# A diffusion backbone layer pair on one core: the feed-forward in two phases, statistics by token half, and seven block products for eight

## The reference, cut to what matters

```
x = x + gate1 * rmsnorm(mixer(modulate(rmsnorm(x))))        # mixer: attention or convolution module
h = modulate(rmsnorm(x))
u = depthwise_conv(h @ w_up, w_dw) + b_dw                   # w_up 1024 x 5632, 3 taps along the tokens
gate, val = split(u, 2)                                     # 2816 channels each
x = x + gate2 * rmsnorm((silu(gate) * val) @ w_down)        # w_down 2816 x 1024

# convolution module
u = a * sigmoid(g)          with a, g = split(h @ w_pw1 + b_pw1, 2)
u = silu(layernorm(depthwise_conv(u, 31 taps) + b_dw))
y = u @ w_pw2 + b_pw2
```

## Time and profile before

| | |
|---|---|
| median of 3 runs | 2824.36 us (2817.53 to 2825.59) |
| profiled execution, its own time | 2821.07 us |
| its span | 2819.3 us |
| PE busy | 2695.0 us, 96% |
| DVE busy | 1663.8 us, 59% |
| ACT busy | 854.7 us, 30% |
| POOL busy | 385.9 us, 14% |
| mean granted clock of PE | 0.976 |
| DMA | 193.96 MB, mean 69 GB/s |

### The profile page before, as it was taken

How to read it: one execution, slowest core, us unless ns; L and a number is a source line. 1 busy time by engine, 2 the same in 40 slices (tenths; PEclk the granted TensorE clock), 3 DMA queues, 4 the chain that set the end, 5 groups by cost and what they waited for, 6 DMA issues and landing times.

```text
span 2819.3 us, 31209 instructions
## 1 busy us (share of the span) xinstructions
PE 2695.0 (96%) x11986; PEld 2134.7 (76%) x11986; DVE 1663.8 (59%) x1770; ACT 854.7 (30%) x1102; POOL 385.9 (14%) x266
## 2 busy tenths in 40 slices
PE   6889999999999999999999999998999999999996
PEld 6667888887758888888887576655678888888884
DVE  5636676767356544554544789995374445444455
ACT  2224444445343222222222422216342222222221
POOL 0402140404025314040400100000100000000001
PEclk9989999999999999999999899999999999999998
DMA  6301120203323212131212200002121111111112
GB/s 245 105 16 50 45 73 21 74 15 109 133 95 112 83 67 97 60 104 52 89 45 104 82 30 30 30 30 82 41 80 60 45 52 45 52 45 52 45 51 106
DMA packets 55063, 193.96 MB, mean 69 GB/s; under 512 B 5840, under 2 KB 7120, under 8 KB 54992
## 3 DMA queue, kind: packets, MB, share of 16 engines
q1 hardware_dynamic: 28048, 99.07, 10.6%
q10 hardware_dynamic: 15424, 51.98, 4.8%
q0 software_dynamic: 11520, 41.95, 4.6%
HBM read 172.00 MB, written 20.97 MB: 68 GB/s over the span
## 4 chain that ended last, share of the span: by engine, by line
PE 89%; DVE 4%; issue 4%; ACT 2%; DMA 1%; POOL 0%; ACTq 0%; POOLq 0%; SPq 0%; DVEq 0%
PE psum L1227 25%; PE psum L1229 25%; PE psum L1228 25%; PE psum L1576 4%; PE psum L1248 2%; PE psum L1448 2%; PE psum L1438 1%; PE psum L1437 1%; PE psum L1235 1%; DVE f32r_region L797 1%; PE psum L1281 1%; DMA f_region<-ctx_t 1%; PE psum L1288 1%; DVE small L925 1%; PE psum L1424 1%
## 5 line engine op out<-in xcount | busy, mean ns | idle before, releaser
L1227 PE MATMUL psum<-f32r_region 128*128 128x512 f32 (+1 forms) x3288 | 1300.1, 395 | 48.9 <-DVE f32r_region L797 13.8
L1228 PE MATMUL psum<-f32r_region 128*128 128x512 f32 (+1 forms) x3288 | 1272.2, 387 | 0.0
L1229 PE MATMUL psum<-f32r_region 128*128 128x512 f32 (+1 forms) x3288 | 1272.0, 387 | 0.0
L1227 PEld LDWEIGHTS psum<-f32r_region 128*128 128x128 f32 x3288 | 624.8, 190 | 197.0 <-issue 32.3
L1228 PEld LDWEIGHTS psum<-f32r_region 128*128 128x128 f32 x3288 | 625.6, 190 | 125.8 <-issue 6.0
L1229 PEld LDWEIGHTS psum<-f32r_region 128*128 128x128 f32 x3288 | 624.6, 190 | 126.3
L384 ACT ACTIVATE f32r_region<-f_region 128x1024 fp32r<-128x1024 f32 (+1 forms) x251 | 254.3, 1024 | 498.1 <-PE psum L1229 446.1
L1095 DVE SCALAR_TENSOR_TENSOR f_region<-psum,vectors,f_region 128x1023 f32<-128x1023 f32 x88 | 112.8, 1282 | 492.3 <-ACT f_region L673 492.3
L673 ACT ACTIVATE f_region<-psum,vectors 128x1024 f32<-128x1024 f32 x88 | 106.2, 1207 | 589.2 <-PE psum L1229 589.2
L1112 DVE TENSOR_TENSOR f_region<-f_region,psum 128x1024 f32<-128x1024 f32 x160 | 194.8, 1217 | 145.9 <-PE psum L1229 145.9
L347 POOL TENSOR_TENSOR f_region<-f_region,f32r_region_plain 128x512 f32<-128x512 f32 x32 | 52.7, 1648 | 1522.8 <-DVE f_region L1055 1522.8
(11 more groups left out here) (108 smaller groups left out, 1853.9 us busy)
## 6 DMA issues: line engine op xcount, KB each, us to landing
f_region<-units SPq DMA_DIRECT2D x178, 512.0 KB, 3.5
f_region<-mod_w POOLq DMA_DIRECT2D x80, 512.0 KB, 3.9
residual<-f_region ACTq DMA_DIRECT2D x24, 512.0 KB, 4.9
f32r_region_plain<-residual ACTq DMA_DIRECT2D x24, 512.0 KB, 7.8
f32r_region_plain<-mod_w ACTq DMA_DIRECT2D x8, 1024.0 KB, 16.3
f_region<-x_t SPq DMA_DIRECT2D x4, 1024.0 KB, 27.9
heads_out<-f_region ACTq DMA_DIRECT2D x16, 256.0 KB, 2.1
f_region<-heads_out ACTq DMA_DIRECT2D x8, 512.0 KB, 4.3
```

The costliest lines, as they stand in the source:

```text
L1227: pe.matmul(out, wl, xh, start=first, stop=False)
L1228: pe.matmul(out, wh, xl, start=False, stop=False)
L1229: return pe.matmul(out, wh, xh, start=False, stop=last)
```

## The change: what it does

**Two phases.** All 22 pairs are made first, each gated block is stored to a tensor `gated` in HBM, and the down-projection follows in four turns: token half 0 with the first four output blocks, then with the last four, then the same for half 1. A turn has 22 steps `j` of 12 matmuls; the sums over `j` stay in PSUM, so DVE's adds (L1112) go. Half units of down weights (256 KB) are loaded in every turn, so each comes twice, and in turns 0 and 2 the gated block's half is read back and split into parts.

**Seven products for eight.** The first three pairs are made directly. For each of the other 19 (MAIN) the 2 x 2 blocks (gate and value rows by two halves of the input channels, on two token halves) are multiplied by seven products in place of eight, each of 4 x 3 matmuls, with sums of weights (s1 to s4, made by POOL for every pair) and of inputs (T1 to T4, made once a layer). PSUM banks a, b, c accumulate; what has to be added across banks is copied out by ACT after its product (`part`), and added by POOL and DVE. The taps of pair p-1 are done in period p, from SBUF.

**Statistics by token half** (`stat_cols`, `stat_spread`): squares of 128x512 are summed over blocks by POOL, and residual, scaling and parts of half 0 go beside PE's work on half 1. The mixers' output projections are made half by half for this, all 8 units of weights at once in SBUF. Modulation vectors are all made during attention, three in a loop trip.

**Convolution.** DVE's gating of the next block (L1189 before, `gated_block`) and the split of two units stand after the twelfth tap of a block, where they stood between two blocks. ACT's copy for the second chain still waits for the end of the block before.

The core of the diff:

```diff
+PRODUCTS = (("gate", 0, "a"), ("s2", 1, "b"), ("s1", 2, "c"), ("s3", 3, "b"), ("gate", 4, "a"), ("s4", 5, "c"), ("val", 6, "b"))
+BANKS = ({"a": 5, "c": 6, "b": 7}, {"a": 1, "c": 2, "b": 3})
...
         @block.gpsimd
+                x, y, op = {1: (a21, a22, ADD), 2: (f(to[0], HALF), a11, SUB), 3: (a11, a21, SUB), 4: (a12, f(to[1], HALF), SUB)}[part]
+                pool.tensor_tensor(f(to[part - 1], HALF), x, y, op).then_inc(s_new, 1)
...
+                for p in range(MAIN):
+                    m = MAIN * layer + p
+                    if p < MAIN - 1:
+                        sums(layer, p + 1, 1, at_sums(p + 1))
+                        sums(layer, p + 1, 2, at_sums(p + 1))
+                    pool.wait_ge(s1_out, 5 * m + 2)
+                    pool.tensor_tensor(f(S_6, HALF), f(S_1, HALF), f(S_6, HALF), ADD).then_inc(u_new, 1)
+                    if p < MAIN - 1:
+                        sums(layer, p + 1, 3, at_sums(p + 1))
+                        sums(layer, p + 1, 4, at_sums(p + 1))
+                    pool.wait_ge(s1_out, 5 * m + 4)
+                    chain(pool.tensor_tensor(f(S_7, HALF), f(S_7, HALF), f(S_1, HALF), ADD))
+                    pool.wait_ge(tap_v, FB * layer + p + 3)
+                    pool.tensor_tensor(f(U_V + HALF, HALF), f(S_7, HALF), f(S_5, HALF), ADD).then_inc(c22_new, 1)
...
         @block.scalar
+                        mid(p + 2, 0, f(U_G))
+                        act.wait_ge(c_new, 2 * m)
+                        act.wait_ge(c22_new, m)
+                        mid(p + 2, 1, f(U_V))
...
+                    part(0, S_1, "a")
+                    silu(p + 2)
...
+                    part(1, S_6, "b")
...
             for i in range(CB):
...
                 if i:
                     act.wait_ge(taps_done, i)
-                copy(f(F_RT), U[i % 2][:, 1:L + 1], V[:, V_WDW + CB + i:V_WDW + CB + i + 1]).then_inc(start_in, 1)
+                copy(f(TAP2), U[i % 2][:, 1:L + 1], V[:, V_WDW + CB + i:V_WDW + CB + i + 1]).then_inc(start_in, 1)
+                if 2 <= i + 1 < CB:
+                    sigmoid(i + 1)
+                    weights_for(i + 1)
...
         @block.vector
+                    def last_quarter(p):
+
+                        dve.wait_ge(mm_done, op_done(layer, p, 6))
+                        dve.wait_ge(s1_out, 5 * (m0 + p) + 1)
+                        dve.tensor_tensor(f(U_V, HALF), f(S_1, HALF), bank(BANKS[p % 2]["b"]), ADD).then_inc(c_new, 1)
+
+                    if p:
+                        last_quarter(p - 1)
+                    taps(p + 2, 0, f(U_G) if p else two(0))
+                    if more:
+                        op_lo(p + 1, 0)
...
+                    taps(p + 2, 1, f(U_V) if p else two(2))
+                    product(p + 2)
+                    if more:
+                        for i in range(1, 6):
+                            op_lo(p + 1, i)
...
+                    dve.wait_ge(mm_done, op_done(layer, p, 5))
+                    dve.wait_ge(u_new, m + 1)
+                    dve.tensor_tensor(f(U_G + HALF, HALF), f(S_6, HALF), bank(bk["c"]), ADD).then_inc(c_new, 1)
+                    if more:
+                        op_lo(p + 1, 6)
...
             for i in range(CB):
-                dve.wait_ge(sig_ready, i + 1)
...
-                split(U_PW1 + 2 * i + 3)
-                split(U_PW1 + 2 * i + 4)
...
                     if t == 12 and i:
                         conv_finish(i - 1)
+                        if i + 1 < CB:
+                            gated_block(i + 1)
...
         @block.tensor
+                        if i in (3, 4, 5, 6):
+                            pe.wait_ge(s1_out, 5 * m + {3: 2, 4: 1, 5: 3, 6: 4}[i])
+                        start = i < 3
+                        for k in range(4):
+                            mm = three(bank(bk[which]), half_unit(op_slot(p, i))[k], operands[i][k], start and k == 0, k == 3, True)
+                        group_done(mm)
+
+                def down(turn, j, c):
+
+                    i = FB * turn + j
+                    if c == 0:
+                        pe.wait_ge(w_lo, w0 + 139 + i + 1)
+                        if turn % 2 == 0:
+                            pe.wait_ge(g_lo, 2 * FB * layer + FB * (turn // 2) + j + 1)
+                    return three(bank(2 * c + turn % 2), half_unit(dn_slot(i))[c], [g_at(j, p) for p in range(2)], j == 0, j == FB - 1)
```

More of the change, by code:

```diff
@@ L605, in fetch @@
[L605 to L631 removed]
+            head_hi(4)
@@ new lines, in norm_part @@
+            def norm_part(half, k):
+                act.wait_ge(t_new, T_BASE["ln", half] + k + 1)
+                act.activation(A_half(k, half), A_half(k, half), ACT.Silu, bias=V[:, V_BLN + k:V_BLN + k + 1]).then_inc(t_act, 1)
+                act.wait_ge(t_act, CB * half + k + 1)
+                copy(h(k, 0, half), A_half(k, half)).then_inc(t_hi, 1)
+            for k in range(CB):
+                centred_square(0, k)
+            std_half()
+            for k in range(5):
+                centred_square(1, k)
@@ L1564, in _, with stat_cols @@
-            ffn(0)
-            boundary(True)
+            def stat_cols(b, half, c):
+                n_stat[0] += 1
+                at = 8 * (n_stat[0] % 2)
+                pe.wait_ge(sq_added, SQ_SUMS[b, half, c])
+                parts = [f(ACC_Y if c == "y" else ACC_X, HALF)] + [ring(SQ_INDEX[b, half, c, k]) for k in (CB - 2, CB - 1)]
+                for n, part in enumerate(parts):
+                    if n:
+                        pe.wait_ge(sq_new, SQ_INDEX[b, half, c, CB - 3 + n] + 1)
+                    for q in range(4):
+                        mm = pe.matmul(bank(STAT, 1, at + q), part[:, q * P:(q + 1) * P], ones[:, 0:1],
+                                       start=n + q == 0, stop=n == 2 and q == 3)
+                mm.then_inc(stat_sums, 1)
@@ new lines, in stat_spread, with group_done, unit_block, halves @@
+            def stat_spread(out, src=DIAG):
+                n_rt[0] += 1
+                pe.wait_ge(stat_diag, n_rt[0])
+                pe.matmul(out, ones[:, :], f(src, HALF), start=True, stop=True).then_inc(stat_rt, 1)
+            def group_done(mm):
+                n_mm[0] += 1
+                return mm.then_inc(mm_done, 1)
+            def unit_block(out, at, k, xs):
+                return three(out, unit(at)[k], xs, k == 0, k == CB - 1)
+            def halves(half):
+                return lambda k: [h(k, p, half) for p in range(2)]
@@ new lines, in ln_sums @@
+            def ln_sums(half, blocks):
+                if blocks[0] == 0:
+                    n_stat[0] += 1
+                at = 8 * (n_stat[0] % 2)
+                for k in blocks:
+                    n = SQ_INDEX["ln", half, "x", k]
+                    pe.wait_ge(sq_new, n + 1)
+                    for q in range(4):
+                        mm = pe.matmul(bank(STAT, 1, at + q), ring(n)[:, q * P:(q + 1) * P], ones[:, 0:1],
+                                       start=k + q == 0, stop=k == CB - 1 and q == 3)
+                    mm.then_inc(stat_sums if k == CB - 1 else sq_one, 1)
```

1630 lines of the change are left out of this document (1111 added, 519 removed).

## The result

The changed kernel took 2707.1 us (median of 4 runs, 2706.24 to 2709.55) against 2822.86 us in the runs of before on the same chip: ratio 0.9594, 95% interval 0.9577 to 0.9610. The forecast was 2707. The total is right to the microsecond, and that is luck: three of its terms were off by 15 to 23 us each and cancelled. (The forecast's change was -117 from 2824; the medians here differ by 115.8.) The profiled execution took 2706.82 us, its span 2705.0, the mean granted clock is 0.967 (0.976 before).

What follows compares the result with a forecast made beforehand. PE's matmul starts bound all stages, and the chain through the statistics about 35 us five times. Terms -103.4 + 19 - 12 - 24 + 1 + 13 - 11 = -117; 2821 - 117 = 2704, plus 3: 2707 us, own range 2680 to 2745.

Steps and rivals of the forecast that it cites:

- The convolution's step: Pointwise-1 and convolution: DVE waits 1.3 us for ACT's copy seven times, period 35.3; stage +13 us, bounds -8 and +25.
- this sign of being wrong: Down-projection: the forecast is wrong if turns 0 and 2 are longer than 1 and 3; DMA was taken as hidden.
- 19.5 a pair, 0.5 over PE: Product pairs: DVE and POOL, one after the other, set a period of 19.5 us against PE's 19.05.
- the +19 us: Product pairs: loss over 38 pairs from DVE and POOL excluding each other; bounds 0 and +75.
- They move and cost nothing: Attention: three modulation sums move into its trips, 1.68 us each wherever they are, with POOL's part costing nothing.
- Into the first feed-forward, 31 against 42.9: Boundary ahead of the first feed-forward, statistics by half: 31 us against 42.9, -12; bounds 0 and -35.
- Into the second, 20 against 43.8: Boundary ahead of the second feed-forward, two sets lying in pointwise-2: 20 us against 43.8, -24; bounds 0 and -35.
- +1: Layer norm and pointwise-2: 37.7 us against 38.2 - 1.5, so +1 us, +-8.
- about 23 us after the last add: Layer norm: matmuls resume about 23 us after the last convolution add, 29 before.
- Tail: After the last matmul, with only half 1 left: 23 us against 34.2, -11, +-5.
- pairs under 19.1: Product pairs: the forecast is wrong if they take under 19.1 or over 20.5 us.
- PE binds everywhere: Rival: no loss in pairs (-19), boundary waits as short as planned (-12), total 2676 us; chance 0.14.

Runs made afterwards that it cites:

- run 3: Changed kernel with ACT's copy for the convolution's second chain going to two buffers in turn, not waiting for the block before: 2705.2 us.
- run 5: Changed kernel with a quarter of the matmuls of each of the seven products left out, 63 for 84 a pair: 2687.1 us.
- run 6: Changed kernel with POOL making nine adds of 128x512 for seven in each pair but the first of a layer: 2737.6 us.
- run 1: Changed kernel with the two modulation sums of each attention trip pulled apart, 16 one-column passes at each place: 2702.0 us, ratio 0.957.
- run 7: Changed kernel with 17 useless matmuls put where PE waits at the convolution's end: 2702.3 us.
- run 9: Run 8's kernel plus 17 useless matmuls keeping PE busy at the convolution's end: 2669.2 us, ratio 0.9470.
- run 8: Changed kernel with modulation sums apart, convolution copy into two buffers and POOL's modulation work started later, all together: 2677.4 us, ratio 0.9499.
- run 4: Changed kernel with POOL's modulation scaling and adding started only after all low parts of the first input: 2684.2 us, ratio 0.952.

## Why the prediction was right or wrong

**What held.** 456 matmuls fewer are 103.4 us: the pair's period is 84c with c at 0.2267, PE never stands in it. The convolution's step held in mechanism and size: a wait of 1.29 us for the copy (1.3 forecast), a period of 35.0 (35.3), and run 3 showed the cause. DMA is hidden (a turn with sets is longer than its neighbours, one without isn't, so this sign of being wrong did not come). The Trainium skill, DMA: Bandwidth & Descriptors, section Bandwidth, spoke against pieces under 1 MiB; the turns of 59.84 us show that here nothing came of it: half units of 256 KB arrive in time. Modulation sums cost 1.68 each where they went.

**"19.5 a pair, 0.5 over PE": mis-sized, 18.6.** That DVE and POOL take turns was right (runs 5 and 6), the +19 us was not: it is 0. The sum was 12.5 + 7.9, less 0.7 for half of the PSUM adds beside POOL and 0.2 for tails. In the timeline just one of the two PSUM adds lies beside POOL, as forecast. DVE's own work, from start to start, is 11.7 us and not 12.3: each start comes some 0.08 us ahead of the last end. POOL's seven adds lengthen it by 6.9 (five low parts of 1.70 from start to start for 0.60, one of 1.11, the product 2.05 for about 1.14), where 7.2 was charged. Together 18.66. An error of 5% in a sum of two engines decided 19 us, because the other side was 19.04. The Trainium skill, GPSIMD Engine Reference, section Specifications (contention with VectorE instructions of two SBUF inputs or in a two-port mode), is borne out: two-input forms are stretched, adds with a PSUM input are not. A one-input scaling of 128x1280 in attention, 0.89 at its shortest, went from 1.06 to 1.55 in the mean of the first trip, which fits the second case, though no row here tells its mode. I had allowed that without the rule the pairs would cost 19 us less. They did cost that much less, with the rule in force.

**"They move and cost nothing": wrong, by 15 us.** The six sums moved at 1.68 each, 10.1. But in the trips the double sum was followed by a lower clock, 12.0 us (run 1), and the opening was 2.2 longer. That POOL's second vector reaches further into DVE's low parts is the likely cause, as with POOL later both kernels stand within 0.7 us of each other (240.64 and 241.31). I had priced a set of passes by its own time and not by what the clock does behind it. The Trainium skill, TensorE: Matmul & The Clock Gate, section HAM oscillation, warns of gaps in which PE stands idle; the rows show a fall with PE busy 12.00 of 12.00 us, so idle gaps are not the only thing to look for.

**Boundaries.** "Into the first feed-forward, 31 against 42.9": the stretch's rest, without the sets in the down-projection, went from 40.3 (856.0 less 3552c and 10.1) to 23.2 (785.9 less 3324c and 9.3), -17 for the -12 forecast: PE hardly waits (2.1 us for the last parts, 3.1 at the entry where I had 5). "Into the second, 20 against 43.8" and layer norm's "+1": together the rest is 79.3 for 80.5, -1 where -23 was forecast. This is the step that failed most. 11 us of it are "about 23 us after the last add": it was 34.1. That sum had DVE's and ACT's work and no passes of PE; the first 64 one-column passes alone took 12.2 us at the lower clock, and 40 more stood ahead of the first product. The waits behind that come to what was forecast, 12.3 for 12, but not where it had them: 7.0 are PE waiting for a bank while ACT is at its silus, which was not in my sum, and 5.3 stand at the parts and the entry. The other 10.6 (32.9 for 22.3) are sets of statistics and the clock: 4.1 for the one set in the down-projection, for which the sum had no term, and most of the rest the clock at the sets, 0.95 over the 111 us from 1909 on. Runs 7 and 9 give the clock's part that can be had back by keeping PE busy: 3.7 and 8.9 us.

**Tail.** 18.9 for 23: root, reciprocal and diagonal took 1.3 us (3 forecast), and what follows POOL's last add 2.4 (4.5).

So +15, -15, -5, +12 and -4 cancelled, and the total of 2707 is no evidence for the single terms. The forecast named "pairs under 19.1" as a sign of being wrong, and that came true; of the rivals, "PE binds everywhere" was right in the pairs and wrong at the second boundary.

**Open.** Why the clock stays lower through layer norm and pointwise-2 when the convolution ends earlier (runs 3 and 8, 0.82 for 0.86) isn't known; that it is the clock is shown by equal busy times of the other engines, and run 9 got it back by filling the waits. Nor is it known why the opening of runs 8 and 9 is 4 us longer than that of run 4. Why some sets of 24 passes are followed by a lower clock and others not was not tried.

## What to carry to other kernels

Where two engines exclude each other, add up their instructions that meet and compare the sum with the engine that binds: the sum here was good to 1 us a pair, which was not enough to tell which side bound. Moving the same POOL work by 34 us, out of the stretch where PE waits for DVE, was worth 23 us (14 in the kernel before, 2817.4 to 2803.8), more than any other edit tried. Price a set of small matmuls by the granted clock of the 10 us behind it, and try two sets apart before putting them together. When a stage that ends in a wait gets shorter, look at the next stage before booking the gain.

## What the runs showed of the hardware

- With 32 one-column passes in a row the granted clock was 0.69 to 0.74 over the 12 us from their start, with PE busy throughout; with 16 at a time it was 1.00 (run 1, three trips). In run 4 it was 0.72, 0.86 and 0.86 after three such sets, so the price isn't fixed.
- 64 passes of one column that follow a busy PE took 11.2 us in run 7 (0.175 each) where 24 in between matmuls took 2.73 (0.114).
- DVE and POOL alternate: five DVE subtractions of 0.68 took 1.72 us each beside POOL adds of 128x512; a DVE instruction with a PSUM input was not touched (0.67). Together they need 18.66 us a pair in the changed kernel's own trace and in run 5.
- Useless matmuls can pay: 17 of them gained 8.2 us in run 9 over run 8; in run 7 the same 17 gained 3.7 us in their stretch, and the total's gain is not clear of noise.
